# A two-part transformer kernel: rotations of queries and keys by copies between partitions, and a new order around the index scores

## The chip, the cores and the metric

The kernel runs on one core of a Trainium2 chip. Its engines are TensorE (PE: matrix products into PSUM), VectorE (DVE), ScalarE (ACT), GpSimd (POOL) and SyncE (SP, which here only issues DMAs). They run side by side, each through its own list of instructions in order, and wait for one another on semaphores. The metric is the device time of one execution in microseconds (us); lower is better.

## The reference

A sequence of 512 tokens with 1024 features goes through a first block (gated linear attention, a short convolution and window attention side by side, then a feed-forward part) and then through two layers of a second block. The change is in those two layers. Each computes, in float32:

```
h = rmsnorm(x);  aq, ak, av, iq, ik, iw, hq, hf, hi, hg, ga, gb = split(h @ w_in)
aq = rope(rmsnorm(aq) * q_norm);  ak = rope(rmsnorm(ak) * k_norm)      8 heads of 64
iq = rope(iq) / 8;  ik = rope(ik);  iw = iw / 2                        4 index heads, 1 index key
rope(v) = concat(v1*cos - v2*sin, v2*cos + v1*sin)                     v1, v2: the halves of a head
score[t, s] = sum over index heads of iw * relu(iq[t] . ik[s]),  s <= t
y_attn = softmax attention of each query over the 128 keys with the highest score
y_hgrn = rmsnorm(gated recurrence of hq, hf, hi, 4 heads of 128) * silu(hg)
x = x + (sigmoid(ga) * (y_attn @ w_a) + sigmoid(gb) * (y_hgrn @ w_h)) @ w_out
x = x + feed-forward(rmsnorm(x))
```

## The kernel before

**Weights.** Every weight matrix is cut into panels of 128 x 2048 numbers (1 MB), 206 in all, listed by `weight_panels` in the order of use. Each panel goes through a ring of three buffers: SyncE loads it (line 918) when the panel three places earlier has been used, ScalarE rounds it to its high part `wh` (956), GpSimd computes the low part `wl` as the difference (940), and TensorE multiplies high and low parts (`products`, 467: three products for each). A projection of one panel takes four quarters (steps), and writes one of two pair buffers in PSUM; the engine that reads the buffer frees it with `pair_free`.

**Side work.** The recurrence (`core`) is a chain over 8 units (4 blocks of 128 tokens x 2 pairs of heads). To keep TensorE busy in it, all engines advance a side generator (`take_on`) at five fixed slots of each unit; `side_core_2` is the side work of the second block, 40 steps, five for a unit. The four engines have their own version of each function, with the same steps. In a unit TensorE computes prefix sums (574), ScalarE exponentiates them (1082), VectorE scales them with queries and keys (1573 to 1581, then `lev_ready`), TensorE multiplies them level by level (595), VectorE collects the results with eight predicated copies (1585, 1595, then `pairs_done`), and TensorE makes the output from them (607).

**Queries and keys.** In `side_core_2` the projections come in the order index key, four pairs of attention queries and keys, index queries, values, gate. For each pair ScalarE squares and copies the product (1294, 1295), TensorE computes the sums over a head (818), and then the rotated halves as a product with a 128 x 128 matrix of ones and minus ones that carries the gain (`turn`, 805; `rot_gain` is made by `turns_with_gains`). VectorE multiplies the result by the sine straight out of PSUM (`sine`, 1959) and adds it to the cosine part (1965, 1968); 1673 to 1974 then normalize. ScalarE makes the mean square (1116) and its inverse root through Ln and Exp.

**After the recurrence.** `index(1)` and `index(2)` (757) compute the index scores of blocks 1 and 2; ScalarE applies ReLU into the one buffer `tmp[3]` (1154), VectorE weights and adds it (1888, 1890) and sends `i_scored`. `select` then takes the highest 128 scores of a query in 16 rounds of MAX8 and MATCH_REPLACE (1900, 1902). `core_post` normalizes the recurrence's output in two halves and multiplies it with the gate's SiLU (1333), with the first steps of the merger (`merge`) between. Then comes `attention`, whose first index work is `index(3)`. The output projection waits for the merged halves (1775).

## Time and profile before

| | |
|---|---|
| median of 3 runs | 2701.91 us (2696.97 to 2702.64) |
| profiled execution, own time | 2704.65 us |
| its span | 2702.8 us |
| mean granted TensorE clock | 0.98 |
| TensorE busy | 2600.1 us, 96% |
| VectorE busy | 1141.3 us, 42% |
| ScalarE busy | 992.8 us, 37% |
| GpSimd busy | 1076.9 us, 40% |
| loaded from HBM | 217.01 MB, 81 GB/s over the span |

In the profile, L467 is line 467 of the kernel, `psum<-uh,wh` says which tile is written from which, and `<-` behind a wait names the instruction that ended it. PE is TensorE's products, PEld its loads of weights, which overlap them; SPq is SyncE's DMA queue. The granted clock is 1.0 at 2.4 GHz and 0.5 at 1.2 GHz. Times in the trace are counted from the start of the span. The first layer of the second block lies at about 940 to 1840 us, the second from there to the end.

### The profile page before, as it was taken

Reading aid. Unit: us, or ns where it says so; the run is one execution under the profiler, and the core shown is the slowest. Engines: PE = TensorE matmul, PEld = TensorE weight load, DVE = VectorE, ACT = ScalarE, POOL = GpSimd, SP = SyncE. Lnnn points to the kernel's source line nnn. Section 1 sums busy time; section 2 is a strip of 40 time slices with the busy share of each in tenths; the row PEclk is TensorE's granted clock in tenths of the full one; section 3 lists DMA queues with packets and bytes.
Section 4 is the critical chain, followed back from the end, with each engine's and each line's share of the span. In section 5 each row is a group of like instructions: output and inputs, shape, how many; then the busy total and the mean of one; then the engine's idle time right before and its main releaser. Section 6 shows DMA issues by size and latency. Waiting matters only on the chain.

```text
span 2702.8 us, 30143 instructions
## 1 busy us (share of the span) xinstructions
PE 2600.1 (96%) x12482; PEld 2112.8 (78%) x12482; DVE 1141.3 (42%) x1977; ACT 992.8 (37%) x1126; POOL 1076.9 (40%) x816
## 2 busy tenths in 40 slices
PE   6998999999999999998999999999999899999998
PEld 4887777888888787876688888888787568888887
DVE  5343353355424466668634111133665863511112
ACT  3422542343323454434424222235443443422220
POOL 3333333645445443213253444443321325444442
PEclk9999999999999999988999999999998999999999
DMA  4222222222232221111132322233111112223222
GB/s 144 75 77 63 94 63 79 94 94 94 94 104 95 86 90 47 50 60 47 48 95 93 106 97 94 94 94 94 48 47 53 57 48 94 94 95 106 95 94 78
DMA packets 206708, 221.05 MB, mean 82 GB/s; under 512 B 3714, under 2 KB 197468, under 8 KB 206444
## 3 DMA queue, kind: packets, MB, share of 16 engines
q1 hardware_dynamic: 206064, 218.97, 25.4%
q8 instruction: 99, 1.62, 0.2%
q14 instruction: 38, 0.30, 0.0%
q10 hardware_dynamic: 507, 0.15, 0.0%
HBM read 217.01 MB, written 2.10 MB: 81 GB/s over the span
## 4 chain that ended last, share of the span: by engine, by line
PE 78%; DVE 14%; ACT 6%; issue 1%; DMA 0%; DVEq 0%; SPq 0%; ACTq 0%
PE psum L467 70%; PE psum L595 2%; DVE score L1902 2%; ACT wh L956 2%; DVE top L1900 2%; DVE ul L1775 1%; DVE tmp L1717 1%; DVE score L1890 1%; DVE dec L1581 1%; PE psum L713 1%; DVE ul L1477 1%; PE psum L574 1%; DVE merged L1798 1%; PE psum L575 1%; PE psum L725 1%
## 5 line engine op out<-in xcount | busy, mean ns | idle before, releaser
L940 POOL TENSOR_TENSOR wl<-raw,wh 128x512 fp32r<-128x512 f32 x812 | 1076.7, 1359 | 1600.0 <-ACT wh L956 1599.6
L467 PE MATMUL psum<-uh,wh 128*128 128x512 f32 x2024 | 811.0, 401 | 25.3 <-DVE ul L1775 4.3
L467 PE MATMUL psum<-ul,wh 128*128 128x512 f32 x2024 | 796.5, 394 | 0.0
L467 PE MATMUL psum<-uh,wl 128*128 128x512 f32 x2024 | 796.5, 394 | 0.0
L956 ACT CAST wh<-raw 128x2048 fp32r<-128x2048 f32 (+1 forms) x206 | 386.9, 1879 | 308.7 <-DMA raw<-in_w_ffn_out 118.1
L467 PEld LDWEIGHTS psum<-uh,wh 128*128 128x128 f32 x2024 | 385.7, 191 | 121.4 <-issue 19.3
L467 PEld LDWEIGHTS psum<-uh,wl 128*128 128x128 f32 x2024 | 385.1, 190 | 82.6
L467 PEld LDWEIGHTS psum<-ul,wh 128*128 128x128 f32 x2024 | 386.1, 191 | 78.5 <-issue 1.0
L467 PE MATMUL psum<-fh,wh 128*128 128x512 f32 x528 | 205.4, 389 | 0.0
L467 PE MATMUL psum<-fh,wl 128*128 128x512 f32 x528 | 205.4, 389 | 0.0
L467 PE MATMUL psum<-fl,wh 128*128 128x512 f32 x528 | 205.4, 389 | 0.0
L1817 DVE TENSOR_TENSOR xT<-xT,psum 128x1024 f32<-128x1024 f32 (+1 forms) x48 | 55.9, 1166 | 293.0 <-PE psum L467 292.8
L1863 DVE TENSOR_TENSOR tmp<-tmp,psum 128x1024 f32<-128x1024 f32 x22 | 26.9, 1221 | 358.6 <-PE psum L467 358.6
L467 PE MATMUL psum<-vh,wh 128*128 128x512 f32 x288 | 115.7, 402 | 9.6 <-DVE xT L2044 7.6
L467 PEld LDWEIGHTS psum<-fh,wl 128*128 128x128 f32 x528 | 99.1, 188 | 20.6
L467 PEld LDWEIGHTS psum<-fl,wh 128*128 128x128 f32 x528 | 99.1, 188 | 20.6
L467 PEld LDWEIGHTS psum<-fh,wh 128*128 128x128 f32 x528 | 99.1, 188 | 20.4
L467 PE MATMUL psum<-vh,wl 128*128 128x512 f32 x288 | 112.9, 392 | 0.0
L467 PE MATMUL psum<-vl,wh 128*128 128x512 f32 x256 | 99.7, 389 | 0.0
L467 PE MATMUL psum<-brh,wh 128*128 128x512 f32 x224 | 91.8, 410 | 1.7 <-ACT tmp L1154 1.7
L467 PE MATMUL psum<-brh,wl 128*128 128x512 f32 x224 | 89.1, 398 | 0.0
L467 PE MATMUL psum<-brl,wh 128*128 128x512 f32 x224 | 89.0, 397 | 0.0
(334 smaller groups left out, 3240.7 us busy)
## 6 DMA issues: line engine op xcount, KB each, us to landing
raw<-in_w_in SPq DMA_DIRECT2D x78, 1024.0 KB, 5.2
raw<-in_w_ffn_in SPq DMA_DIRECT2D x44, 1024.0 KB, 5.1
raw<-in_w_up SPq DMA_DIRECT2D x22, 1024.0 KB, 5.1
raw<-in_w_ffn_out SPq DMA_DIRECT2D x16, 1024.0 KB, 5.1
raw<-in_w_down SPq DMA_DIRECT2D x8, 1024.0 KB, 5.0
raw<-in_w_out SPq DMA_DIRECT2D x8, 1024.0 KB, 5.1
raw<-in_w_ffn_out SPq DMA_DIRECT2D x8, 768.0 KB, 4.4
raw<-in_w_o SPq DMA_DIRECT2D x4, 1024.0 KB, 5.0
```

The costliest lines, as they stand in the source:

```text
L467: ins = mm(dst, x, y, start=first and i == 0, stop=last and i == len(todo) - 1)
L574: mm(X[1 + b][:, 0:3 * P], lth[:, u % 2, i, :], summask[:, cols], start=True, stop=False)
L575: ins = mm(X[1 + b][:, 0:3 * P], ltl[:, u % 2, i, :], summask[:, cols], start=False, stop=True)
L595: ins = mm(level_scores(l)[:, i, :, :], dec[:, i, l, :], odd_blocks(dec[:, i, l, :], l), start=True, stop=True)
L713: ins = nc.tensor.transpose(X[2][:, c * P:(c + 1) * P], prob[i % 2][:, e, b * P:(b + 1) * P], ident)
L725: ins = mm(X[3][HD * e:HD * (e + 1), 0:P], vof(2 * p + e, b), probT[i % 2][:, e, (b - b0) * P:(b - b0 + 1) * P], start=(b == b0), stop=(b ...
L940: ins = nc.gpsimd.tensor_tensor(wl[p % 3][:, w], raw[p % 3][:, w], wh[p % 3][:, w].bitcast(F32), ALU.subtract)
L956: nc.scalar.copy(wh[p % 3][:, 0:nk * width], raw[p % 3][:, 0:nk * width]).then_inc(S.hi_done, 1)
L1477: v.tensor_tensor(dst, src, high.bitcast(F32), ALU.subtract).then_inc(sem, 1)
L1817: v.tensor_tensor(x, x, src, ALU.add).then_inc(pair_free[(n.q - 1) % 2], 1)
L1900: v.max(top8[:], sc).then_inc(S.dve_chain, 1)
L1902: v.match_replace(sc, top8[:], sc, TAKEN).then_inc(S.dve_chain, 1)
```

## The change

- **Rotations by copies.** The products of `turn` are gone. SyncE copies each half of a head to the partitions of the other half (`turn_halves`: four DMAs of 32 partitions each for a pair, 128 KB each, into `tmp[2]`; for the index queries and keys four and four, 768 KB). It does so after it has issued the next panel load, once ScalarE has emptied the product and VectorE has used up the previous copy (`rope_done`). The sign and the gain, turned once at the start by a product of five columns, are applied in `sine`, which waits for the copies on `turned`.
- **Order.** The index queries are projected right after the index key; `index(1)`, its ReLU and its weighting stand in `side_core_2`; both ReLU tiles of a block have their own place (`index_tiles`), so that the ReLU no longer waits for the weighting. `indexed_post` takes the place of `core_post` in the second block: first normalization, second gate projection, `index(2)`, two merger steps, second normalization, four merger steps. Of the 25 selection rounds that were in `core_post`, 16 are in `side_core_2` and 9 in `indexed_post`; 23 stay in `attention`.
- **GpSimd held back.** `low_after` lets the low part of certain panels start only when VectorE has sent the unit's last `lev_ready` (in both recurrences), or the last `m_lo` (in the output projections).

```diff
-                  C_IK, C_AQ, C_AQ + 256, C_AK, C_AK + 256, C_IQ, C_AV, C_AV + 256, C_HG):
+                  C_IK, C_IQ, C_AQ, C_AQ + 256, C_AK, C_AK + 256, C_AV, C_AV + 256, C_HG, C_HG + 256):
             cols(w, c)
-        merge(w, C_G2 + D, a["w_proj_hgrn_2"][l], C_HG + 256)
+        merge(w, C_G2 + D, a["w_proj_hgrn_2"][l])
...
-SIDE_POST_2 = (4, 2)
+SIDE_POST_2 = (2, 4)
...
-SELECT_EARLY = (15, 10)
+SELECT_CORE, SELECT_POST = (8, 8), 9
...
+        def index_tiles(m):
+            if m == 1:
+                return [tmp[3][:].rearrange("p a (b t) -> p (a b) t", b=2)[:, 2 * j:2 * j + 2, :] for j in range(2)]
+            return [(rectified[0] if m == 2 else tmp[3])[:, :, 0:(m + 1) * P], rectified[1][:, :, 0:(m + 1) * P]]
...
+            def hold_lows(first, sem):
+                for p in range(first, ended()):
+                    if p + 3 < n_panels:
+                        low_after[p + 3] = (sem, t.at[sem.name])
...
+                    hold_lows(free, S.lev_ready)
                     take_on(side, core_steps(total, u, 2))
                     take_on(side, core_steps(total, u, 3))
+                    free = ended()
...
+            def indexed_post(side, side_steps):
+                sum_heads()
+                finish(project(uh, ul))
+                index(2)
+                take_on(side, side_steps[0])
+                sum_heads()
+                take_on(side, side_steps[1])
+                pe.wait_ge(S.g_mean, t.up(S.g_mean, 2))
...
+                low_after[last + 3] = (S.m_lo, t.at["m_lo"])
...
-            def turn(src, by):
-
+            def side_core_2():
+                yield from project(uh, ul, (0,))
+                yield from project(uh, ul)
+                turn_after[n.p - 1] = (-1, n.q - 1)
                 dst = new_pair()
-                for i in range(src.shape[1]):
-                    ins = mm(dst[:, i, :], by, src[:, i, :], start=True, stop=True)
+                for m in range(NT):
+                    ins = nc.tensor.transpose(dst[:, 1, 4 * m:4 * m + 4], iwT[:, m * P:(m + 1) * P], ident[HD:HD + 4, HD:HD + 4])
                 ins.then_inc(S.pair_full, 1)
-
-            def side_core_2():
-
-                yield from project(uh, ul, (0,))
-                keys = n.q - 1
+                yield
                 for j in range(4):
                     yield from project(uh, ul)
-                    mine = n.q - 1
+                    turn_after[n.p - 1] = (j, n.q - 1)
                     dst = new_pair()
                     pe.wait_ge(S.squared, t.up(S.squared))
                     for i in range(2):
                         ins = mm(dst[:, i, :], blk, qksq[:, i, :], start=True, stop=True)
                     ins.then_inc(S.pair_full, 1)
-                    pe.wait_ge(pair_free[mine % 2], mine // 2 + 1)
-                    turn(qk_pair[j], rot_gain[j // 2])
                     yield
-                yield from project(uh, ul)
-                queries = n.q - 1
-                dst = new_pair()
-                pe.wait_ge(pair_free[keys % 2], keys // 2 + 1)
-                for m in range(NT):
-                    nc.tensor.transpose(dst[:, 1, 4 * m:4 * m + 4], iwT[:, m * P:(m + 1) * P], ident[HD:HD + 4, HD:HD + 4])
-                mm(dst[:, 0, :], rot, ik[:], start=True, stop=True).then_inc(S.pair_full, 1)
-                yield
                 yield from project_tokens()
-                pe.wait_ge(pair_free[queries % 2], queries // 2 + 1)
-                turn(iq, rot)
+                index(1)
...
+            def turn_halves(dst, src):
+                for c in range(0, P, HD):
+                    sp.dma_start(dst[c:c + HD // 2], src[c + HD // 2:c + HD]).then_inc(S.turned, 16)
+                    sp.dma_start(dst[c + HD // 2:c + HD], src[c:c + HD // 2]).then_inc(S.turned, 16)
...
+                if p - 3 in turn_after:
+                    j, q = turn_after[p - 3]
+                    sp.wait_ge(pair_free[q % 2], q // 2 + 1)
+                    if j < 0:
+                        sp.wait_ge(pair_free[(q - 1) % 2], (q - 1) // 2 + 1)
+                        turn_halves(tmp[1][:, 0, :], ik[:])
+                        turn_halves(tmp[2][:], iq[:])
+                    else:
+                        sp.wait_ge(S.rope_done, t.up(S.rope_done))
+                        if j == 3:
+                            t.up(S.rope_done)
+                        turn_halves(tmp[2][:], qk_pair[j])
...
+                if p in low_after:
+                    pool.wait_ge(*low_after[p])
...
+            def rectify(m, j):
+                src = next_pair()
+                act.wait_ge(S.pair_full, n.q)
+                fn(index_tiles(m)[j], src[:, :, 0:(m + 1) * P], ACT.Relu).then_inc(pair_free[(n.q - 1) % 2], 1)
+                ahead()
+            def indexed_post(side, side_steps):
+                def root_heads():
+                    act.wait_ge(S.g_summed, t.up(S.g_summed))
+                    mean_square(tmp[1][:], X4[:, 0:2, :], 1.0 / P, S.g_mean)
+                    act.wait_ge(S.g_mean, t.up(S.g_mean))
+                    logarithm(tmp[2][:], tmp[1][:])
+                root_heads()
                 act.wait_ge(S.i_scored, t.up(S.i_scored))
+                inverse_root(tmp[2][:]).then_inc(S.g_root, 1)
+                silu_gate(silu1[:])
+                rectify(2, 0)
+                high_branch(0)
+                rectify(2, 1)
+                act.wait_ge(S.out_read, t.up(S.out_read))
+                square_heads(1)
+                take_on(side, side_steps[0])
+                root_heads()
+                act.wait_ge(S.g_split, t.up(S.g_split))
+                inverse_root(tmp[2][:]).then_inc(S.g_root, 1)
+                take_on(side, side_steps[1] - 2)
+                high_branch(1)
+                take_on(side, 2)
...
+                yield from evict(iq[:])
+                src = next_pair()
+                act.wait_ge(S.pair_full, n.q)
+                fn(iw[:].rearrange("p m h -> p (m h)"), src[:, 1, 0:4 * NT], ACT.Copy,
+                   scale=1.0 / 16).then_inc(pair_free[(n.q - 1) % 2], 1)
+                ahead()
...
+                rectify(1, 0)
+                rectify(1, 1)
...
+                square_heads(0)
+                silu_gate(tmp[0][:])
...
+            def indexed_post(g, side, side_steps, selection):
+                gate_heads(0, g, True, tmp[0][:])
+                next_pair()
+                score_keys(2)
+                take_on(selection, SELECT_POST)
+                take_on(side, side_steps[0])
+                gate_heads(1, g, True, silu1[:])
+                take_on(side, side_steps[1])
...
-                def sine(dst):
-                    src = next_pair()
-                    dve.wait_ge(S.pair_full, n.q)
-                    v.tensor_tensor(dst, src, sinT[:].unsqueeze(1).to_broadcast([P, 2, T]),
-                                    ALU.mult).then_inc(pair_free[(n.q - 1) % 2], 1)
-                    dve.wait_ge(pair_free[(n.q - 1) % 2], (n.q - 1) // 2 + 1)
+            def side_core_2(l, selection):
+                def sine(c, copies):
+                    dve.wait_ge(S.turned, t.up(S.turned, 16 * copies))
+                    v.scalar_tensor_tensor(tmp[2][:], tmp[2][:], small[:, c:c + 1], sinT[:].unsqueeze(1).to_broadcast([P, 2, T]),
+                                           ALU.mult, ALU.mult).then_inc(S.dve_chain, 1)
...
+                weights = n.q - 1
+                sine(54, 8)
+                yield
+                yield from wait_steps(2)
+                dve.wait_ge(pair_free[weights % 2], weights // 2 + 1)
+                v.scalar_tensor_tensor(ik[:], tmp[1][:, 0, :], small[:, 54:55], sinT[:], ALU.mult, ALU.mult).then_inc(S.dve_chain, 1)
+                dve.wait_ge(S.dve_chain, t.up(S.dve_chain))
+                v.tensor_tensor(ik[:], ik[:], ikcos[:], ALU.add).then_inc(S.dve_chain, 1)
+                dve.wait_ge(S.dve_chain, t.up(S.dve_chain))
+                dve.wait_ge(pair_free[queries % 2], queries // 2 + 1)
+                v.tensor_tensor(iq[:], iq[:], cosT[:].unsqueeze(1).to_broadcast([P, 2, T]), ALU.mult).then_inc(S.dve_chain, 1)
+                dve.wait_ge(S.dve_chain, t.up(S.dve_chain))
+                v.tensor_tensor(iq[:], iq[:], tmp[2][:], ALU.add).then_inc(S.rope_done, 1)
...
-                    sine(tmp[2][:])
+                    sine(50 + 2 * l + j // 2, 4)
                     yield
                     yield from wait_steps(2)
                     cosines(j)
                     yield
                     normed(j)
-                    if j < 3:
-                        next_pair()
-                        yield
-                src = next_pair()
-                dve.wait_ge(S.pair_full, n.q)
-                v.tensor_copy(iq[:], src).then_inc(pair_free[(n.q - 1) % 2], 1)
-                dve.wait_ge(pair_free[(n.q - 1) % 2], (n.q - 1) // 2 + 1)
-                yield
-                src = next_pair()
-                dve.wait_ge(S.pair_full, n.q)
-                v.tensor_scalar(iw[:].rearrange("p m h -> p (m h)"), src[:, 1, 0:4 * NT], 1.0 / 16, None, ALU.mult)
-                v.tensor_tensor(ik[:], src[:, 0, :], sinT[:], ALU.mult).then_inc(pair_free[(n.q - 1) % 2], 1)
-                dve.wait_ge(pair_free[(n.q - 1) % 2], (n.q - 1) // 2 + 1)
-                v.tensor_tensor(ik[:], ik[:], ikcos[:], ALU.add).then_inc(S.dve_chain, 1)
-                dve.wait_ge(S.dve_chain, t.up(S.dve_chain))
+                    next_pair()
...
+                score_keys(1)
                 yield
                 yield from wait_steps(2)
-                cosine(iq[:])
+                take_on(selection, SELECT_CORE[0])
                 yield
                 yield from passed(1)
-                sine(iq[:])
-                v.tensor_tensor(iq[:], iq[:], tmp[2][:], ALU.add).then_inc(S.rope_done, 1)
-                dve.wait_ge(S.rope_done, t.up(S.rope_done))
+                yield from wait_steps(3)
+                next_pair()
+                take_on(selection, SELECT_CORE[1])
```

## Rows read from the trace of the kernel before

**Rows 1.** The profile's page: the span, and TensorE's busy time.
```profile
span 2702.8 us, 30143 instructions
...
PE 2600.1 (96%) x12482; PEld 2112.8 (78%) x12482; DVE 1141.3 (42%) x1977; ACT 992.8 (37%) x1126; POOL 1076.9 (40%) x816
```

**Rows 2.** TensorE's waits, whole run: waiting line <- releaser: us in total, times, longest.
```profile
PE psum L595 <- DVE dec L1581: 6.7, 6, 1.9
PE psum L757 <- ACT tmp L1154: 5.5, 4, 1.4
...
PE psum L467 <- ACT tmp L1154: 4.5, 4, 1.4
...
PE psum L467 <- DVE ul L1775: 4.3, 3, 1.5
...
PE psum L757 <- ACT tmp L1333: 3.6, 2, 1.8
...
PE psum L467 <- ACT tmp L1116: 2.7, 2, 1.3
```

**Rows 3.** Rotation products by source line and tile: duration ns min/median/max, first and last start.
```profile
L805 PE MATMUL psum<-aq,const x16: 592/592/593, 1032.5 to 1944.8; 128*128 128x512 f32 x16
...
L805 PE MATMUL psum<-iq,const x8: 592/593/595, 1147.7 to 2029.4; 128*128 128x512 f32 x8
...
L829 PE MATMUL psum<-ik,const x4: 592/644/697, 1127.8 to 2008.8; 128*128 128x512 f32 x4
```

**Rows 4.** Timeline, first layer, units 1 and 2: start us, duration us, engine, line.
```profile
1047.44 2.58 DVE L1595 COPY_PREDICATED attT<-pairmask,psum 128x128 f32<-128x128 uint8 x7
...
1059.95 0.34 PE L574 MATMUL psum<-summask,lth 128*128 128x384 f32 x1
...
1060.14 0.37 SPq L918 DMA_DIRECT2D raw<-in_w_in  x1
...
1061.07 1.01 ACT L1295 ACTIVATE aq<-psum 128x1024 f32<-128x1024 f32 x1
1061.32 1.95 PE L818 MATMUL psum<-qksq,const 128*128 128x512 f32 x4
...
1063.11 1.88 PE L805 MATMUL psum<-aq,const 128*128 128x512 f32 x4
...
1067.33 1.21 DVE L1959 TENSOR_TENSOR tmp<-psum,sinT 128x1024 f32<-128x1024 f32 x1
...
1074.11 0.38 PE L607 MATMUL psum<-attT,gv 128*128 128x128 f32 x2
```

**Rows 5.** DMA issues on SyncE's queue: count, KB each, median us from issue to landing.
```profile
raw<-in_w_in SPq DMA_DIRECT2D x78, 1024.0 KB, 5.2
...
out<-xtok SPq DMA_DIRECT2D x4, 512.0 KB, 2.7
```

**Rows 6.** Windows: length, busy us of PE, PEld, DVE, ACT, POOL, granted clock, DMA.
```profile
1182.00:1236.00 54.00, 44.89 (x161) 31.14 (x162) 40.80 (x97) 30.30 (x27) 15.32 (x12) 0.81 0.19 59
1236.00:1262.00 26.00, 21.77 (x88) 14.16 (x86) 18.82 (x42) 11.10 (x21) 6.83 (x5) 0.80 0.14 41
203.00:214.00 11.00, 8.23 (x31) 6.51 (x30) 8.73 (x12) 1.98 (x3) 5.21 (x4) 0.73 0.31 95
```

**Rows 7.** Timeline, first layer, unit 1: GpSimd's low halves and VectorE's scalings.
```profile
1033.35 10.48 POOL L940 TENSOR_TENSOR wl<-raw,wh 128x512 fp32r<-128x512 f32 x8 [13.23 <-ACT wh L956]
...
1038.79 1.36 DVE L1581 TENSOR_TENSOR dec<-dec,gk 128x128 f32<-128x128 f32 x1
...
1044.10 0.28 DVE L1581 TENSOR_TENSOR dec<-dec,gq 128x128 f32<-128x128 f32 x1
```

**Rows 8.** Timeline of VectorE, first layer: two rounds of the selection.
```profile
1199.61 0.43 DVE L1900 MAX8 top<-score 128x8 f32<-128x256 f32 x1
...
1200.60 0.43 DVE L1900 MAX8 top<-score 128x8 f32<-128x256 f32 x1
```

**Rows 9.** Timeline of ScalarE, first layer: the table load ahead of the gate's SiLU.
```profile
1185.14 1.28 ACT L1333 ACT_TABLE_LOAD   x1 [10.09 <-PE psum L467]
```

More of the change, by code:

```diff
@@ L369, in build_program @@
         qksq = at("qksq", 69, [P, 2, T])
-        rot_gain = [const[:, K_DIST + i * P:K_DIST + (i + 1) * P] for i in range(2)]
         prob = [tmp[0], tmp[1]]
@@ L461, in new_pair, with ended @@
                 return pair[(n.q - 1) % 2]
+            def ended():
+                return sum(1 for end in panel_end if end)
+            def hold_lows(first, sem):
+                for p in range(first, ended()):
+                    if p + 3 < n_panels:
+                        low_after[p + 3] = (sem, t.at[sem.name])
             def products(dst, terms, first, last):
@@ L558, in core @@
                     n.fresh = 0
+                free = ended() - 1
                 for u in range(CORE_UNITS):
@@ L777, in output @@
                 n.fresh = S.m_lo
-                residual(uh, ul)
+                last = ended() - 1
+                finish(project(uh, ul))
+                low_after[last + 3] = (S.m_lo, t.at["m_lo"])
+                for s in range(1, DC // 2):
+                    finish(project(uh, ul))
             def ffn(bare):
@@ L2103, in _ @@
                 dve.wait_ge(S.dve_chain, t.up(S.dve_chain))
+            for l in range(LAYERS):
+                for i, g in enumerate(gains_of(l)):
+                    v.tensor_copy(small[:, 45 + 2 * l + i:46 + 2 * l + i], g).then_inc(S.dve_chain, 1)
+                    dve.wait_ge(S.dve_chain, t.up(S.dve_chain))
+            v.memset(small[:, 49:50], 1.0).then_inc(S.dve_chain, 1)
+            dve.wait_ge(S.dve_chain, t.up(S.dve_chain))
             angle, turns = tmp[3][:, 0, :], tmp[3][:, 1, :]
```

185 lines of the change are left out of this document (91 added, 94 removed).

## The prediction

> **What bounds the kernel now.** I read the busy times on the page first: TensorE is busy 2600.1 us of a span of 2702.8 [rows 1], so the time can only fall by giving TensorE less to do or by closing its gaps; the busy shares of the other engines matter only where TensorE waits for them. Then the list of TensorE's waits over the whole run [rows 2], which says which gaps exist. Leaving out the start, the largest are 6.7 us for the scaled decays (line 1581), 5.5 and 4.5 us for the ReLU of the index scores (1154), 4.3 us for the low half of the merged branch (1775), 3.6 us for the SiLU of the gate (1333) and 2.7 us for the mean square (1116). Then the windows [rows 6], because a gap is followed by a stretch at a lower granted clock. In the 54 us between the end of the first layer's recurrence and its first attention product TensorE is idle 54 - 44.9 = 9.1 us and the granted clock is 0.81 (1.0 is 2.4 GHz, 0.5 is 1.2 GHz): (1 - 0.81) x 54 = 10.3 us of clock are missing, part of it inside the idle time. That stretch loses between 10 and 19 us per layer. The next 26 us lose 4.2 us idle and up to 5.2 us of clock.
>
> **Part 1: the products with the rotation matrix go.** Every rotation of a pair was four records of 592 ns each (16 for the queries in both layers, 16 more alike for the keys, 8 for the index queries, 4 for the index keys [rows 3]). The records overlap; from start to start of the two groups in a unit (1061.32, for the means, to 1063.11, for the rotation) four take 1.79 us, 0.447 each [rows 4]. 44 records x 0.447 = **19.7 us**, all on TensorE, so all on the path. The one new product (five columns) and the seven small VectorE copies and a memset at the start are each some 0.2 to 0.3 us; two multiplications per layer that prepared the rotation matrices go. I take nothing, with 0 to 1.5 us for the range. The pair buffer of the rotation also goes: the next projection then takes the buffer that ScalarE has already emptied, not that of the means. The 2.7 us of waits for line 1116 [rows 2] go too: **2.7**.
>
> **Part 2: what takes their place.** SyncE, after it has issued the load of panel p, waits until ScalarE has copied the product out, then issues 4 copies of 128 KB (8 copies, 768 KB, for index queries and keys). What stands behind that wait on SyncE is only the next panel's load, whose own release is the end of a projection four quarters later; so nothing is late there. VectorE waits for the landing where it used to read the rotation's product. Behind this wait in its queue stand the predicated copies of the decayed scores, and TensorE waits for these before the output product of line 607. So the cost is: landing + sine + predicated copies, against TensorE's arrival. With T = 1059.95, the end of the projection of unit 2 in the first layer [rows 4]: ScalarE's copy out (1061.07, 1.01 us) ends at T+2.1; the panel load was issued at T+0.2 and takes 5.2 us to land, on the same queue. A 512 KB store took 2.7 us from issue to landing [rows 5], of which I take 1.5 to 2.7 as coming on top of the load: the turned halves land at T+6.9 to T+8.1. VectorE finishes its scalings only at 1067.33, T+7.4 [rows 4], so most of the transfer is hidden by work that it must do anyway. Then the sine, 1.21 us, and eight predicated copies, seven of which took 2.58 us [rows 4], 3.1 together, ending at T+11.7 to T+12.4. TensorE came to line 607 at 1074.11, T+14.2; without the rotation's 1.8 us it comes at T+12.4. Slack is 0 to 0.7 us: the transfer is just hidden, and anything above T+8.1 is paid one for one.
> The sine read PSUM before and reads on-chip memory twice now, while GpSimd's subtraction for the panel just cast starts at the same time. A scaling with two such operands took 1.36 us beside GpSimd and 0.28 without [rows 7], so this can add up to 1.1 us. The Trainium skill has the rule for it ("SBUF — State Buffer", on the shared port pair: a VectorE instruction with two SBUF inputs and a GpSimd one shut each other out for the whole instruction); the trace agrees, 1.36 against 0.28 us. Taking 0.4 us for each of 8 rotations and 1 for each of 2 index rotations, where the means no longer give time and 768 KB move, makes **-5**. Ends: 0, and 3 us for each of ten, -30.
> Against the change speaks another sentence of the same page (section "Door 1: The DMA port swizzle"): a transfer touching 32 partitions reaches 8 of 16 ports, 189 against 328 GB/s at 1 MiB. The trace cannot show it, all its large transfers touch 128 partitions. By it, as an estimate, a 512 KB rotation moves in 2.8 instead of 1.6 us, 1.2 us later each time, or some 10 us in all, and the forecast would be 2663.
>
> **Part 3: the order around the index scores.** Before, TensorE computed the index scores of blocks 1 and 2 one after the other with one buffer (`tmp3`) between ScalarE's ReLU and VectorE's weighting, and waited for each. This chain, and the SiLU ahead of it, hold 5.5 + 4.5 + 3.6 us of waits [rows 2]. Now block 1 is done inside the recurrence, block 2 after the second gate projection, with separate buffers, and 16 of the selection rounds go into the recurrence. A round is 0.99 us (1199.61 to 1200.60 [rows 8]), so 15.8 us of VectorE's work leave the stretch where it is busy 40.8 of 54 us [rows 6] and go where it waits; each batch of eight (7.9 us) stands at the end of a unit, and the next scalings are not due before the next sums. Not all of the 10 to 19 us comes back: index block 2's second half waits for a SiLU behind a table load of 1.28 us [rows 9] (some 1 us left), the next projection for a ReLU behind a panel cast (1.4 by the same reckoning), the block moved into the recurrence brings a wait of 1, and the second normalization ends on VectorE about when attention wants it. Of 15 lost I keep 6: **9 per layer, 18**; ends 5 and 13 per layer. At the opening of attention the index scores of block 3 lose the same ping-pong: **2 per layer, 4** (0 to 4 each).
>
> **Part 4: GpSimd held back.** A panel's low half now waits for the scalings (or the merged low half). GpSimd idles most of the time, and a low half is needed only when two more panels have been used, so a hold of a few us delays nobody. It takes GpSimd off VectorE's scalings: in the first block the stretch 203:214 lost 2.8 us idle and 3.0 of clock [rows 6], 5.8 together, nearly all of it by scalings beside GpSimd: **6**. In unit 1 of each layer GpSimd ran 10.5 us over two panels and VectorE's scalings took 1.36 us each [rows 7]; only the second of these panels is held, so I count half of the 6.7 us [rows 2] and some clock: **4**. For the merged halves, half of 4.3 [rows 2]: **2**.
>
> **The sum** against the profiled run's own 2704.65 us: 19.7 + 2.7 + 18 + 4 + 6 + 4 + 2 - 5 = 51.4, so 2653.3. The profiled run is 2.7 us above the median of the three, 2701.91, which I leave inside the rounding: **2653 us**, 1.8% faster. A measurement here tells about 0.2% (5 us) from no change.
>
> **Rivals.**
> *The transfers land late.* Four copies in a row behind a panel load are not in the trace; if they land 3 us after the point where they are hidden, ten times, 25 us more than the sum has are lost: 2678. For it: slack of under 1 us. Against: VectorE's own scalings cover the first 7.4 us. (The skill's sentence on the 8 ports points this way.)
> *The gaps only move.* VectorE's second normalization, or ScalarE with its table loads between Ln, Exp and SiLU, becomes last after the recurrence; part 3 gives 2 instead of 22 and the rest holds: 2673. For it: VectorE is busy 40.8 of 54 us there [rows 6]. Against: 15.8 us of that leave.
> *All gaps close:* parts 3 and 4 at their upper ends, +18: 2635.
> *Slower than before:* each of the ten units has a gap ahead of line 607 that also brings the clock down. At 203:214 a gap of 2.8 us cost 3.0 us of clock besides [rows 6], so a gap costs about twice itself. The 51.4 us are used up when each unit loses 5.1 us more than I count, a gap of 2.6 us, that is a landing from about T+11 on. At T+12 it is 7.2 us a unit, 72 in all where I have 5: 2720.
> *The change doesn't do what it says:* the code removes the products in both layers, so I give this no chance.
>
> **Chances.** Forecast 0.58 (2640 to 2666), late transfers 0.16 (2666 to 2692), gaps move 0.12 (2664 to 2682), all gaps close 0.08 (2628 to 2640), slower 0.06. From these, faster by over 0.2% 0.92, within 0.2% 0.03, slower 0.05. The range reaches up over most of the two milder rivals and down into the better one: 2634 to 2682.
>
> **What would show it.** Right: no records with the rotation matrix other than one, TensorE's busy time down by about 20 us, the wait of line 1116 gone, the copies landing within 8 us of the projection's end, and the granted clock at 0.9 or more in the 50 us before attention. Wrong: waits of TensorE for the last predicated copy in units 1 to 5 of each layer, with VectorE idle before the sine; or the stretch after the recurrence as long as before with VectorE's second normalization at its end. GpSimd's low halves late would show as waits of line 467 for `wl`.

## The result and the profile after

The changed kernel takes 2686.88 us (median of 6, 2679.98 to 2691.97) where the kernel before takes 2701.01 (median of 6): a ratio of 0.9941, 95% interval 0.9922 to 0.996. It is faster by 0.6%. Forecast were 2653 us and a range of 2634 to 2682. The profiled execution has a span of 2686.2 us and an own time of 2688.3, 16.4 under the 2704.65 before; the sum had 51.4.

The page of the changed kernel, its span and its busy times, beside [rows 1]:

```profile
span 2686.2 us, 30127 instructions
...
PE 2575.9 (96%) x12440; PEld 2102.2 (78%) x12440; DVE 1152.2 (43%) x1975; ACT 994.3 (37%) x1130; POOL 1084.5 (40%) x816
```

TensorE's busy time fell by 24.2 us, as it should. The span fell by 16.6. So TensorE now waits 7.6 us longer than before, and its list of waits says for whom (columns as in [rows 2]):

```profile
PE psum L740 <- DVE stat L1808: 11.9, 2, 6.4
PE psum L631 <- ACT kdt L1138: 11.8, 8, 1.7
PE psum L760 <- DVE inverse L1829: 7.8, 2, 4.1
...
PE psum L488 <- DVE ul L1866: 4.4, 3, 1.5
PE psum L682 <- DVE cdec L1725: 3.9, 2, 2.1
```

The second line is new: eight waits for ScalarE's copy of `kdt` (the turned keys, for which TensorE waits ahead of the unit's output products), one in each unit that carries a query or key pair. The wait of line 1116 is gone. The last two lines, for the low half of the merged branch and for the scalings of the first block, are where they were, 4.3 and 3.9 us before.

Three stretches tell where the time went. I measure them between starts of TensorE's records: the recurrence of a later layer from its first prefix sums to its last key-value product, then to the second query-key product of attention, then to the last one. For each, first and second of the two layers, us:

| | recurrence | to 2nd q-k product | to last q-k product |
|---|---|---|---|
| before | 175.7, 176.2 | 61.9, 61.9 | 82.1, 82.2 |
| after | 177.9, 177.7 | 51.2, 51.2 | 82.9, 83.1 |

In the recurrence 22 of the 44 rotation records left each layer (22 x 0.447 = 9.8 us) and index block 1 came in (8 products, 1.14 us, 1.9 until the next projection begins): some 8 us less work, and it takes 2 us longer. The opening of attention gave 10.7 us a layer. These stretches sum to -16.0 us over both layers; the rest of the kernel holds the remaining 0.6.

The second gain shows in the window from the last key-value product to the second query-key product of the first layer, which answers to the first row of [rows 6] (same columns):

```profile
1182.97:1234.15 51.18, 43.77 (x182) 33.01 (x180) 40.69 (x77) 27.74 (x25) 16.49 (x12) 0.96 0.27 83
```

The granted clock is 0.96 of 2.4 GHz where it was 0.81, so of 10.3 us of missing clock 2 are left; 7.4 us of idle time are.

### The profile page after: what moved, and what is told of

Same layout as the page of the kernel before. It is cut to its first block, busy times and chain, and to the rows that moved or that the text cites. A ratio compares the mean times of both kernels' runs of the same rounds, so it can differ in the third digit from the quotient of the medians.

```text
span 2686.2 us, 30127 instructions
## 1 busy us (share of the span) xinstructions
PE 2575.9 (96%) x12440; PEld 2102.2 (78%) x12440; DVE 1152.2 (43%) x1975; ACT 994.3 (37%) x1130; POOL 1084.5 (40%) x816
## 4 chain that ended last, share of the span: by engine, by line
PE 78%; DVE 11%; ACT 7%; DMA 3%; issue 1%; POOL 0%; DVEq 0%; SPq 0%; ACTq 0%
PE psum L488 71%; DMA raw<-in_w_in 2%; ACT wh L1006 2%; DVE score L1987 1%; DVE top L1985 1%; PE psum L617 1%; PE psum L751 1%; DVE ul L1866 1%; PE psum L740 1%; DVE score L1975 1%; PE psum L763 1%; DVE merged L1889 1%; DVE tmp L1808 0%; PE psum L596 0%; DVE normed L1620 0%
## 5 line engine op out<-in xcount | busy, mean ns | idle before, releaser
L488 PEld LDWEIGHTS psum<-uh,wh 128*128 128x128 f32 x2024 | 383.8, 190 | 110.9 <-issue 15.2
L1954 DVE TENSOR_TENSOR tmp<-tmp,psum 128x1024 f32<-128x1024 f32 x22 | 26.9, 1221 | 357.3 <-PE psum L488 357.2
L488 PEld LDWEIGHTS psum<-fh,wl 128*128 128x128 f32 x528 | 99.1, 188 | 20.7
L488 PEld LDWEIGHTS psum<-fh,wh 128*128 128x128 f32 x528 | 99.1, 188 | 20.6
```

The source lines that it names most:

```text
L488: ins = mm(dst, x, y, start=first and i == 0, stop=last and i == len(todo) - 1)
L1954: v.tensor_tensor(tmp[2][:], tmp[0][:], src, ALU.mult).then_inc(pair_free[(n.q - 1) % 2], 1)
```

## Experiments

**What bounds a unit with a query or key pair?** The timeline of unit 2 of the first layer in the changed kernel, with T = 1057.05, the end of the projection (start us, duration, engine, line, idle time before it and its releaser):

```profile
1057.05 0.34 PE L596 MATMUL psum<-summask,lth 128*128 128x384 f32 x1
...
1063.25 1.90 ACT L1006 CAST wh<-raw 128x2048 fp32r<-128x2048 f32 x1 [1.72 <-DMA raw<-in_w_in]
1065.17 1.28 ACT L1169 ACT_TABLE_LOAD   x1
...
1065.84 1.74 DVE L2043 SCALAR_TENSOR_TENSOR tmp<-tmp,small,sinT 128x1024 f32<-128x1024 f32 x1 [1.32 <-DMA tmp<-aq]
...
1068.10 2.61 DVE L1677 COPY_PREDICATED attT<-pairmask,psum 128x128 f32<-128x128 uint8 x7
...
1070.89 0.35 ACT L1138 COPY kdt<-psum 128x256 f32<-128x256 f32 x1
1071.39 0.46 PE L631 MATMUL psum<-attT,gv 128*128 128x128 f32 x2 [1.70 <-ACT kdt L1138]
```

The same rows of the kernel before, where T is 1059.95:

```profile
1065.46 1.92 ACT L956 CAST wh<-raw 128x2048 fp32r<-128x2048 f32 x1 [1.03 <-DMA raw<-in_w_in]
...
1073.11 0.35 ACT L1088 COPY kdt<-psum 128x256 f32<-128x256 f32 x1
```

ScalarE makes the mean, then waits for the next panel and casts it (`ahead()` in the code), then runs logarithm, exponential and square with two table loads, then copies `kdt`. Before, that copy ended at T+13.5, 0.65 us ahead of TensorE's arrival at T+14.16. So with this copy where it was, TensorE could gain at most 0.65 of its 1.79 us. In the changed kernel the panel's cast begins at T+6.2 instead of T+5.5, `kdt` is copied at T+14.2, and TensorE starts line 631 at T+14.34, later than before. VectorE's masks end at T+13.66: second last, by half a microsecond. From here two theories: A, ScalarE's chain holds the units and TensorE's time is free there; B, TensorE's time counts and the loss is elsewhere.

*TensorE's time doubled back.*

```
-for i in range(2):
+for i in (0, 1, 0, 1):
     ins = mm(dst[:, i, :], blk, qksq[:, i, :], start=True, stop=True)
```

> TensorE makes the products with blk (the means of the squares) of the four query and key pairs twice, so that each of the 8 units that hold one carries 4 more matmul records of 0.447 us, 1.79 us, just what the rotation products took there; 14.3 us of work over both layers, results unchanged. Theory A (in these 8 units ScalarE's copy of kdt and VectorE's masking end last, so TensorE's time there is free): the wait before L631 for kdt, 1.70 us in a unit and 11.8 us in all 8, falls to near zero, and the time grows by 0 to 4 us over the changed kernel. Theory B (TensorE's time counts in these units, and the gain of the change was lost elsewhere): the time grows by 12 to 15 us. As a ratio to the changed kernel: A 1.000 to 1.0015, B 1.0045 to 1.0055.

Measured: 2686.57 us, ratio to before 0.9934 (0.9915 to 0.9954) against 0.9941; recurrence 177.3 and 178.1 us. One wait for `kdt` of 0.5 us is left of the eight. The eight units together take 1.4 us more (178.5 for 177.1), the whole kernel no more than the changed kernel does: theory A. 14.3 us of TensorE's work were next to free, so the products that had been removed there were worth next to nothing in the changed kernel.

*The panel's cast behind the copy of `kdt`* (the same `ahead()` leaves `rooted`):

```
 mean_square(tmp[1][:], src, 1.0 / HD, pair_free[mean % 2])
-ahead()
...
 nc.scalar.copy(kdt[:], ...).then_inc(S.kdt_done, 1)
+ahead()
```

> ScalarE's cast of the next panel's high part, which waits 1.72 us for the panel's landing and then runs some 1.9 us between the mean and the logarithm of each query and key unit, is moved behind the copy of kdt. Nothing else changes. Theory A (ScalarE's chain ends the unit last): kdt is copied some 3.5 us earlier, VectorE's masking (its end at T+13.7, 0.6 us ahead of TensorE's start of L631) ends last instead; the 8 units gain 0.5 to 1.5 us each, 4 to 12 us in all, less what GpSimd's later split costs the next unit's scalings. Theory B (the copy of kdt is only the later of several and VectorE's chain ends as late): under 2 us. Rival C (the later split of the low part collides with the scalings of the next unit, as in unit 1): slower by 2 to 10 us, with the waits for cdec, dec or attT grown.

Measured: 2670.95 us, ratio 0.9879 (0.9858 to 0.9899), 16 us under the changed kernel by the medians; recurrence 169.5 and 172.0, 14 us less. The eight units themselves, all at a granted clock of 1.00 in both profiles, take 166.4 us for 177.1: 10.7 us, 1.3 a unit, which is theory A's. The rest of the 16 is not explained by the move; 3 us of it lie in units outside the eight that take one of two lengths in any of these kernels (see the last section). Timeline of unit 2, T = 1052.51:

```profile
1061.04 1.28 DVE L2043 SCALAR_TENSOR_TENSOR tmp<-tmp,small,sinT 128x1024 f32<-128x1024 f32 x1 [1.06 <-DMA tmp<-aq]
...
1062.73 0.35 ACT L1138 COPY kdt<-psum 128x256 f32<-128x256 f32 x1
1062.84 2.61 DVE L1677 COPY_PREDICATED attT<-pairmask,psum 128x128 f32<-128x128 uint8 x7
...
1065.50 0.49 PE L631 MATMUL psum<-attT,gv 128*128 128x128 f32 x2 [0.35 <-DVE attT L1677]
```

`kdt` is ready at T+10.6, VectorE's masks are last, and TensorE starts at T+13.0 instead of T+14.3. GpSimd's split also begins later, behind the sine, and the sine takes 1.28 us at the median of 10 instead of 1.96.

*The same addition to that kernel.*

> late_cast, with the products for the means made twice as in double_means: 14.3 us more of TensorE's work in the 8 units. In late_cast TensorE comes to L631 at T+12.65 and waits 0.35 us for attT, so it is the last or nearly so. Theory A: now TensorE's work counts, 1.45 to 1.79 us a unit, 11 to 15 us over late_cast: 2682 to 2686, where the same addition cost the changed kernel nothing (2686.6 against 2686.9). Theory B (TensorE has slack in these units in any case): under 4 us over late_cast.

Measured: 2686.82 us, ratio 0.9929 (0.991 to 0.9948), 16 us over late_cast by the medians; recurrence 177.7 and 179.3. The eight units take 176.9 us for 166.4: of 14.3 us added, 10.5 arrive, 1.3 a unit where the changed kernel had 0.2. In these units TensorE's time counts when ScalarE's chain does not end last, and hardly otherwise.

*The same move in the kernel before.*

> The kernel before the change with the same move of ScalarE's panel cast behind the copy of kdt as in late_cast. There kdt is copied by T+13.5 and TensorE comes to L607 at T+14.2 without a wait. Theory A (the change took 1.8 us from TensorE and so made ScalarE's chain the last of the unit; before, TensorE was last): nothing to gain, ratio to before 1.000, within 0.002. Theory B (late_cast gained by something of its own, less of GpSimd's contention for example, which the kernel before would gain as well): 10 to 16 us faster, ratio 0.994 to 0.996.

Measured: 2694.5 us, ratio 0.9961 (0.9944 to 0.9978), 11 us faster by the medians. The size is theory B's; the place is not. The distances of the key-value products in units 2 to 4 are 22.0 to 22.1 us as before, which is theory A's. The gain lies in unit 1, 24.0 instead of 30.6 and 31.0 us, and is of the kind that theory B gave as its example, less contention with GpSimd. It is no part of what late_cast gained over the changed kernel, where unit 1 has its hold already (25.5 and 26.9 us against 27.0 and 26.9). GpSimd's low halves in unit 1, beside [rows 7]:

```profile
1033.38 5.37 POOL L940 TENSOR_TENSOR wl<-raw,wh 128x512 fp32r<-128x512 f32 x4 [13.22 <-ACT wh L956]
...
1043.59 5.02 POOL L940 TENSOR_TENSOR wl<-raw,wh 128x512 fp32r<-128x512 f32 x4 [4.84 <-ACT wh L956]
```

The second panel is cast later, so it no longer runs beside the scalings. The granted clock in unit 1 is 1.00, where it was 0.89 and 0.83. By this profile the collision was worth 6.6 us in one layer and 7.0 in the other; the sum had read 6.7 us of waits for both layers together [rows 2] and kept half of them.

*No turning copies* (the rotated halves of queries and keys are not computed):

```
-if p - 3 in turn_after:
+if False:
...
-dve.wait_ge(S.turned, t.up(S.turned, 16 * copies))
+dve.wait_ge(pair_free[mine % 2], mine // 2 + 1)
```

> The turning copies of SyncE are left out, with the waits for them: VectorE multiplies what lies in tmp[2] and tmp[1] as soon as the pair is copied, so the rotated halves of the queries and keys are not computed. 5.8 MB less moved, 36 DMA issues fewer, and the sine step starts some 1.3 us or more earlier in a unit. Theory A (ScalarE's chain, which waits for the panel's landing and not for the copies, ends the unit last): the time falls by 0 to 4 us, and TensorE's wait before L631 stays near 1.5 us in a unit. Theory B (the landing of the copies ends the unit last, by way of VectorE): the wait before L631 is gone and the time falls by 8 to 14 us. The landing of a panel, 5.3 us with the copies and 5.2 us before the change, should stay within 0.3 us.

Measured: 2676.85 us, ratio 0.9894 (0.9873 to 0.9915), 10 us under the changed kernel by the medians (48 DMA issues fewer, not 36); recurrence 172.2 twice, 5.6 us a layer less. The timeline, T = 1054.32:

```profile
1059.74 1.90 ACT L1006 CAST wh<-raw 128x2048 fp32r<-128x2048 f32 x1 [0.94 <-DMA raw<-in_w_in]
...
1067.38 0.35 ACT L1138 COPY kdt<-psum 128x256 f32<-128x256 f32 x1
1067.88 0.46 PE L631 MATMUL psum<-attT,gv 128*128 128x128 f32 x2 [0.92 <-ACT kdt L1138]
```

The wait for `kdt` stays (6.9 us in 8), so the copies did not hold the unit through VectorE. They held it through the panel: its cast starts at T+5.4 without them and T+6.2 with them, and everything of ScalarE's behind it moves by those 0.8 us. The eight units take 172.1 us for 177.1: 5.0 us are the copies'. Theory A had 0 to 4 and kept the wait, theory B had 8 to 14 and no wait left, so A's account holds. Another 6 us of the recurrences lie in the first, second and last units. Unit 1, with the 768 KB, takes 25.5 us for 27.0 and 26.9, but it also takes 25.5 us in the first layer of branch_first below and 26.8 in the second, with the copies in both; so these 6 us are not shown to be the copies'. My expectation for theory A missed this, since it looked at the median landing of all panels, which is 5.3 against 5.2 us.

*Copies first, then the panel's load*, on top of late_cast: for a query or key pair `sp.dma_start(wview(raw, p), src)` moves from ahead of `turn_halves` to behind it.

> As the run late_cast, and SyncE issues the four turning copies of a query or key pair ahead of the load of the next panel instead of behind it; the load is issued some 3.7 us later. If VectorE's chain from the landing of the copies (sine, cosine, sum, root, masks) ends the unit last once the cast is out of the way, the earlier copies (by up to 0.7 us of one issue, the rest held by ScalarE's copy of the pair) give 0 to 5 us over late_cast. If VectorE is held by what stands ahead of the sine (the scalings end at T+7.5 and the sine starts at T+8.8), no more than 1 us a unit can come of it. If the later load delays the cast and the low part that TensorE needs three panels on, nothing shows before 60 us are used up; so no loss from that is expected.

Measured: 2672.79 us, ratio 0.9878 (0.9856 to 0.9899), the same as late_cast. Units 2 to 5 take 20.3 to 20.6 us, which is the 22.1 of before less 1.8 (unit 5 carried no pair before): there the whole forecast gain is seen. But unit 6 grows to 25.2 and 25.5 us (23.0 in late_cast): TensorE waits 2.8 us there for VectorE's masks, where it was 1.7, and the granted clock is 0.95 for 1.00. The casts come later in this run, which is a likely cause; no run separates it.

**The opening of attention.** TensorE's second query-key product still waits 5 to 6 us, for VectorE. The chain in the first layer of the changed kernel:

```profile
1203.98 1.90 ACT L1006 CAST wh<-raw 128x2048 fp32r<-128x2048 f32 x1 [1.46 <-DMA raw<-in_w_proj_hgrn]
1205.78 1.04 ACT L1189 CAST brh<-tmp 128x1024 fp32r<-128x1024 f32 x1
1206.93 2.30 DVE L1559 TENSOR_TENSOR brl<-tmp,brh 128x1024 fp32r<-128x1024 f32 x1 [5.60 <-ACT brh L1189]
...
1214.71 0.56 DVE L1985 MAX8 top<-score 128x8 f32<-128x384 f32 x1
...
1217.61 1.06 ACT L1176 ACTIVATE tmp<-tmp 128x1024 f32<-128x1024 f32 x1
...
1225.96 1.22 DVE L1755 TENSOR_TENSOR tmp<-tmp 128x1024 f32<-128x1024 f32 x1
...
1234.15 0.80 PE L740 MATMUL psum<-ak,aq 64*128 64x128 f32 x4 [5.47 <-DVE stat L1808]
```

VectorE idles 5.6 us for `brh`, behind two panel casts on ScalarE; then nine rounds run from 1214.71 to 1225.96 while the root has been ready since 1218.7.

*Fewer rounds there*:

```
-SELECT_CORE, SELECT_POST = (8, 8), 9
+SELECT_CORE, SELECT_POST = (8, 8), 2
```

> Two selection rounds of block 2 instead of nine stand between the index scores and the second gate normalization on VectorE; the other seven go into the rounds spread over attention (30 over 11 head pairs instead of 23). In the changed kernel the root for the second normalization is ready some 8 us before VectorE comes to it, and TensorE's second attention product (L740) waits 6.4 us in a layer (11.9 in two). Theory A (the rounds are what holds it): that wait falls to under 2 us and the time by 8 to 14 us. Rival B (the seven rounds, 7 to 8 us a layer, come back one for one in attention, where VectorE also ends last): the wait moves, the stretch from the second to the last query-key product grows from 83 to about 90 us and the total stays within 4 us. Rival C (what is late next is the root or GpSimd beside the normalization): 3 to 7 us.

Measured: 2692.71 us, ratio 0.9953 (0.9935 to 0.997). The opening takes 45.7 and 44.5 us (51.2), the rest of attention 92.2 twice (82.9, 83.1): 6 gained and 9 lost. Rival B, and a little worse: the seven rounds gave 5.5 and 6.7 us and cost 9.2, so they stood in a good place already.

*`brh` ahead of the two casts* (with `False` the two helpers leave out their `ahead()`):

```
-silu_gate(silu1[:])
-rectify(2, 0)
+silu_gate(silu1[:], False)
+rectify(2, 0, False)
 high_branch(0)
+ahead()
```

> After the recurrence ScalarE makes the high half of the gated branch (brh) before, not behind, the two panel casts of 1.9 us, the second of which waits 1.5 us for its landing. In the changed kernel VectorE idles 5.6 us for brh. Theory A (VectorE's chain brh, low half, index scores, nine rounds, normalization sets the start of attention): the chain comes 3 to 4 us earlier, TensorE's wait of 6.4 us at L740 shrinks by as much in each layer, 5 to 8 us in all. Rival B (the casts, now later, hold the next projection for its low half, a wait of L488 for wl): the wait at L740 shrinks but one for wl appears, total within 3 us.

Measured: 2675.8 us, ratio 0.9891 (0.9871 to 0.991). The opening takes 47.0 us in both layers, 4.2 less, and attention is unchanged; the wait at L740 falls from 11.9 to 6.5 us. No new wait for `wl` appears. Theory A. The median fell by 11 us, of which the two openings explain 8.4.

*joined*: late_cast, branch_first and fewer_post, and the index scores of block 1 weighted a step later.

> The late cast (run late_cast, 2671 us), with the two edits fewer_post and branch_first, and with the index scores of block 1 weighted on VectorE one step later, behind the masking of unit 6 instead of ahead of it (there, in late_cast, TensorE waits 1.7 us for attT and the unit takes 23.0 instead of 21 us). The pieces lie in different stretches, so if each is worth what its stretch says (2 us a layer for the scores, 7 to 9 a layer for the opening of attention, less up to 7 a layer for the rounds that go into attention) the time is 2648 to 2664. Above 2667 VectorE's rounds in attention take it all back.

Measured: 2675.46 us, ratio 0.9892 (0.9869 to 0.9915): above the line drawn; fewer_post takes back its share (attention 92.2 us again), and the later weighting moved nothing (unit 6 takes 23.0 us as in late_cast).

**GpSimd's holds.** *Without them*:

```
-if p in low_after:
-    pool.wait_ge(*low_after[p])
```

> GpSimd's low halves are no longer held behind the scalings (lev_ready) or the merged low half (m_lo). By the trace of the changed kernel the holds catch nothing of the collision in the first block (POOL starts at 204.59 beside the scalings, released by the cast, and TensorE waits 3.9 us for cdec as before) and half of the one in unit 1 of each later layer. If so, the time grows by 0 to 5 us, all of it in unit 1. The prediction's terms for the holds (6 + 4 + 2) would make it 12 us slower.

Measured: 2693.23 us, ratio 0.9959 (0.9944 to 0.9974). Unit 1 takes 30.2 and 31.0 us instead of 27.0 and 26.9: the hold there gives 3.2 and 4.1 us. The second layer's first unit is longer too, 21.2 us for 16.4, with a wait of 2.2 us for the masks, which the expectation had not. The first block's and the merged waits are the same with and without (3.9 and 4.4 us). Why the first block got nothing (changed kernel, first block):

```profile
204.59 5.22 POOL L990 TENSOR_TENSOR wl<-raw,wh 128x512 fp32r<-128x512 f32 x4 [11.68 <-ACT wh L1006]
...
208.62 1.35 DVE L1725 TENSOR_TENSOR cdec<-cdec,gk 128x128 f32<-128x128 f32 x1
```

The low half is released by the cast, not by the hold: the hold names the unit in which the buffer came free, and ScalarE casts a unit later. *All holds of the first block one unit on*:

```
-hold_lows(free, S.lev_ready)
+hold_lows(free, S.lev_ready, 2 if u + 1 < CORE_UNITS else 0)
...
-low_after[p + 3] = (sem, t.at[sem.name])
+low_after[p + 3] = (sem, t.at[sem.name] + later)
```

> In the first block's recurrence the low half of a panel is held until the scalings of the unit after the one in which the panel's buffer came free, since ScalarE's cast comes a unit later than the hold supposes (POOL 204.59 beside the scalings at 206.29 to 208.62, 1.1 to 1.4 us each). If the hold was only tied to the wrong unit, the two waits for cdec, 2.1 and 1.8 us, go, with some clock: 4 to 8 us off the changed kernel's time (the prediction had 6 for this term). Rival: GpSimd now collides with what follows the scalings (predicated copies, the side's own operations) or comes too late for its panel: no gain, within 3 us, and a new wait for att or wl.

Measured: 2694.59 us, ratio 0.996 (0.9944 to 0.9975). The waits for `cdec` are gone, but a panel that needed no hold came late:

```profile
PE psum L488 <- POOL wl L990: 12.9, 3, 9.5
```

*Only the two panels that collide*:

```
-low_after[p + 3] = (sem, t.at[sem.name])
+low_after[p + 3] = (sem, t.at[sem.name] + (2 if p + 3 in (14, 16) else 0))
```

> Only the two panels whose low halves ran beside the scalings of the first block (POOL at 204.59 and 241.10 in the changed kernel) are held one unit further, so that they follow those scalings; the others stay as they were. Theory A (the term of 6 us was right and the hold only released a unit early): the waits for cdec (2.1 and 1.8 us) go, no wait for wl comes, 4 to 7 us off the changed kernel. Rival (the collision moves on to the predicated copies and to the state's update, or the 4 us come back at the next wait): within 3 us.

Measured: 2681.18 us, ratio 0.9902 (0.9885 to 0.9918). The first block's two colliding units take 15.2 and 17.0 us instead of 20.7 and 20.8, the stretch behind them, to the first score product of the window attention, 63.0 instead of 61.4: 7.7 us. The term of 6 had about the right size against this profile and the wrong code behind it; against a profile whose clock did not fall there it is less, as the next step shows.

**Put together.** late_cast with branch_first, and then with hold_two as well:

> late_cast and branch_first together. They lie in different stretches (units 2 to 5; behind the recurrence): late_cast took 12 to 16 us off the changed kernel and branch_first 4.2 us a layer by the stretch between the last kv product and the second query-key product (51.2 to 47.0). If they add up: 2671 less 8, 2659 to 2666, in the range of what was forecast for the change itself. If the opening of attention is bound by something that late_cast already moved, 2668 to 2672.

Measured: 2658.5 us (4 runs, 2657.63 to 2664.73), ratio 0.9832 (0.9815 to 0.985). The openings take 47.0 us, the recurrences 170.6 and 169.6. The two gains add up (28 us by the medians, for 16 and 11), to within 6 us of the time that was forecast for the change.

> late_cast_branch (2658.5 us) with the two holds of hold_two. If the pieces add up, 4 to 7 us less, 2651 to 2655, which is the time forecast for the change. If the first block's term is worth nothing, 2656 to 2661.

Measured: 2660.54 us, ratio 0.9823 (0.9807 to 0.9839), not to be told from late_cast_branch, where 4 to 7 us were expected; the two units take 15.2 and 17.0 us here too. In late_cast_branch's profile they take only 18.0 and 19.3 (see the last section), so the holds had 2.8 + 2.3 - 1.6 = 3.5 us to give there.

## Why the prediction was wrong, by its steps

**Part 1, the rotation products (19.7) and line 1116 (2.7).** The work went, by 24.2 us of busy time with all that went with it. "All on TensorE, so all on the path" is the step that failed: I took a busy engine without a wait for one whose time counts, and did not look at how far behind it the next engine was. In the 89 us from the start of unit 2 of the kernel before TensorE is busy without a gap, and in the changed kernel it has 6 us of gaps:

```profile
1060.00:1148.70 88.70, 88.70 (x522) 75.20 (x521) 57.90 (x140) 46.76 (x47) 20.36 (x16) 1.00 0.17 50
```

```profile
1057.00:1146.00 89.00, 82.97 (x498) 71.16 (x498) 64.75 (x140) 53.31 (x52) 23.93 (x16) 1.00 0.26 72
```

The row of `kdt`'s copy, T+13.5, was in the trace of before and would have capped the gain at 0.65 us a unit, 5.2 in all. double_means shows that of the 1.8 us a unit next to nothing arrived. Of the other 12 records, the index rotations' (5.4 us of the 19.7), no run says what they were worth.

**Part 2, the copies (-5).** The chain that I priced, landing, sine, masks, was right in kind: the copies landed at T+8.8 instead of T+6.9 to T+8.1, the sine took 1.96 us at the median, inside the bounds (10 x 0.7 us more than 1.27), and the masks ended at T+13.66 where I had T+12.4 at the latest. The failed step is the list of who waits: "landing + sine + predicated copies, against TensorE's arrival" leaves out ScalarE, which waits for the panel on the same DMA queue and has two table loads and `kdt` behind that wait. That wait, not VectorE's, is where the copies were paid: 5.0 us in the eight units by no_copies, and 10 in all by the medians. The sum had 5, so its size may well be right, by luck, since it was made up of the sine's longer duration on a path that did not end last. On the Trainium skill's two statements from "SBUF — State Buffer": the shared port pair shows, the sine takes 1.27 us without GpSimd beside it and up to 2.37 with it. Of the section "Door 1: The DMA port swizzle" I had made 1.2 us a rotation, 2663 in all. The copies of 32 partitions landed 4.2 us after their issue, and the delay that counted was 0.8 us a unit, on the landing of the panel ahead of them; no run used wider copies, so the rule itself stays untested.

**Part 3, the order around the index scores (18 and 4).** The stretch to the second query-key product gave 10.7 us a layer. The index block that moved into the recurrence is 1.1 to 1.8 of them (1.14 us here, 0.70 and 1.06 us of busy time there), and attention gave 0.8 and 0.9 back instead of 2 forward, so the two terms are worth some 17 us, not 22: 21.4, less 1.7 in attention, less the 1.1 to 1.8 a layer of moved work. The missing part is the rival that I had priced as "the gaps only move", in a mild form: VectorE's second normalization did end last, behind nine rounds and a 5.6 us wait for `brh`. That `brh` stands behind two casts, one with a wait for a landing, could be read from the new order on ScalarE; I looked only at the queue of VectorE.

**Part 4, the holds (6, 4 and 2).** First block 0 instead of 6: the mechanism was right, and hold_two shows 7.7 us for it by one pair of profiles and 3.5 by another, but I took the code's hold to reach the panel that collides without comparing the unit it names with the unit of the cast. Unit 1 gave 7.3 us by the two profiles instead of 4. The merged halves gave nothing (4.4 us against 4.3).

By stretches the miss is some 22 us in the recurrences, 5 in the opening and attention, 6 in the first block and 2 at the merged halves, together the 35 between 51.4 and 16.4. A few of the 22 may be chance: branch_first, fewer_post and hold_two have the same recurrence in the later layers, and theirs take 350.8, 351.8 and 357.1 us over both, for 355.6 here. The two repairs of ScalarE's order bring the time to 2658.5; the two milder rivals, "late transfers" (2678) and "gaps move" (2673), each came true in part, together with a third that I had not named (ScalarE's chain inside the units), and the range, drawn as if one alone could come true, ended at 2682.

## What to carry to other kernels

When work is taken from the engine that never waits, read for each place where the next engine stands: the difference is all that can be gained there, and if it is under the removed time, the order on the second engine has to change with it. Follow every engine's queue behind a wait that the change delays, above all casts that wait for a landing ahead of something small and urgent, and issue extra transfers with the load in mind that shares their queue. Compare stretches that ran at the same granted clock before giving a difference of a microsecond or two to an edit. A hold must name the event that it is meant to follow in the unit where the held work really starts.

## What the runs showed of the hardware

The same collision in the first block costs two different amounts in kernels whose code there is the same. After an equal gap, 2.10 us of TensorE's for the scalings, the granted clock fell to 0.84 in one and stayed at 1.00 in the other; first the products behind the gap, in the changed kernel and in late_cast_branch, then the window that holds them, in the same order (columns as in [rows 6]):

```profile
210.02 2.07 PE L682 MATMUL psum<-cdec 128*128 128x128 f32 x8 [2.10 <-DVE cdec L1725]
```

```profile
208.46 1.38 PE L682 MATMUL psum<-cdec 128*128 128x128 f32 x8 [2.10 <-DVE cdec L1728]
```

```profile
209.00:230.00 21.00, 19.98 (x91) 16.96 (x92) 8.21 (x20) 4.77 (x6) 3.11 (x3) 0.84 0.16 51
```

```profile
209.00:230.00 21.00, 21.00 (x109) 17.69 (x108) 6.65 (x18) 4.76 (x6) 5.03 (x4) 1.00 0.16 51
```

The colliding units take 20.7 and 20.8 us with the drop and 18.0 and 19.3 without. The prediction's rule that "a gap costs about twice itself" holds in some executions only. What decides it was not found. Unit 1 of the later layers shows the same inside one execution. The two windows are unit 1 of the first and of the second layer in late_cast:

```profile
1020.04:1045.51 25.47, 22.23 (x111) 19.02 (x110) 11.87 (x29) 7.50 (x8) 11.25 (x8) 0.87 0.26 73
1885.70:1912.55 26.85, 23.61 (x110) 20.46 (x109) 11.85 (x29) 7.50 (x8) 11.23 (x8) 0.81 0.25 69
```

The first unit of a layer likewise takes 16.4 us at 1.00 or 18.0 at 0.91, the last 21.2 at 1.00 or some 22.6 at 0.93. So profiles can differ by several us in recurrences with the same code, and a gain of 1.5 us in such a unit says nothing about the edit. Units 2 to 5 stood at 1.00 in all kernels on whose sums I rely above.

A copy of 128 KB between partitions takes SyncE 0.5 to 0.6 us to issue and lands 4.2 us after that (the queries'), or 4.1 (the keys'), against 2.7 us for a 512 KB store [rows 5]:

```profile
tmp<-aq SPq DMA_DIRECT2D x16, 128.0 KB, 4.2
tmp<-ak SPq DMA_DIRECT2D x16, 128.0 KB, 4.1
```
